# Neighbourhood attention: two heads at a time on both halves of the array, negated logits, and two pairs of logits moved into the value projection

## What is computed

```python
def row_block(r):                       # each of the 4 rows of the 64-wide grid
    rs = jnp.clip(r - kh // 2, 0, rows_n - kh)
    s_nb = jnp.einsum('bchd,bicjhd->bhcij', q_r, k_win).reshape(B, NA_HEADS, GRID_W, kh * NA_KW)
    s_nb = s_nb + bias[None]
    s_cx = jnp.einsum('bchd,blhd->bhcl', q_r, k_c)
    p = jax.nn.softmax(jnp.concatenate([s_nb, s_cx], axis=-1).astype(jnp.float32), axis=-1)
    ...
    return jnp.einsum('bhcij,bicjhd->bchd', p_nb, v_win) + jnp.einsum('bhcl,blhd->bchd', p_cx, v_c)
```

## Time and profile before

| | us |
|---|---|
| median of three runs | 2557.35 (2555.93 to 2558.05) |
| the profiled execution | 2556.38 |
| its span, first to last instruction | 2554.7 |
| first score matmul to first matmul of the output projection | 935.62 to 1032.93 |
| PE busy in the span | 2092.2 (82%) |
| DVE busy | 910.2 (36%) |
| ACT busy | 674.2 (26%) |
| DMA, mean over the span | 232 GB/s, and 418 GB/s from 1700 to 2550 |

### The profile page before, as it was taken

One profiled execution on the slowest core, in us unless ns is written; L12 is line 12 of the kernel. 1 busy time (PEld: TensorE's weight loads), 2 busy tenths in 40 slices (PEclk: granted clock), 3 DMA queues, 4 the chain that ended last, 5 costly groups with the idle time before them and its releaser, 6 DMA issues.

```text
span 2554.7 us, 37430 instructions
## 1 busy us (share of the span) xinstructions
PE 2092.2 (82%) x16374; PEld 1521.7 (60%) x16374; DVE 910.2 (36%) x1632; ACT 674.2 (26%) x1171; POOL 56.3 (2%) x83
## 2 busy tenths in 40 slices
PE   6997998999998989999989999666666666666655
PEld 4895645888776875799879445533344343333332
DVE  2335623444423227466365533423311111211112
ACT  4234313233314326455355211111111111111111
POOL 0011100000000011000000000000000000000000
PEclk8998999999998989999989999788878888888888
DMA  7107741222222321153631035599999999999997
GB/s 318 67 34 299 299 180 51 95 99 79 68 101 99 117 100 48 70 195 126 222 134 42 1 155 197 228 427 427 426 427 427 427 426 427 427 427 426 427 427 298
DMA packets 44433, 592.11 MB, mean 232 GB/s; under 512 B 5528, under 2 KB 5717, under 8 KB 8176
## 3 DMA queue, kind: packets, MB, share of 16 engines
q1 hardware_dynamic: 40608, 579.36, 55.5%
q0 software_dynamic: 2880, 8.45, 1.0%
q10 hardware_dynamic: 784, 1.91, 0.2%
HBM read 588.64 MB, written 1.05 MB: 231 GB/s over the span
## 4 chain that ended last, share of the span: by engine, by line
PE 53%; DMA 27%; DVE 4%; ACT 2%; issue 2%; SPq 0%; POOL 0%; DVEq 0%; ACTq 0%
DMA s_ring<-in_w_up 12%; PE bank L510 10%; PE bank L511 10%; PE bank L512 10%; DMA s_arena<-in_w_up 8%; PE bank L1079 5%; DMA s_hT<-in_w_up 4%; DMA s_xT<-in_w_up 3%; PE bank L1093 2%; PE bank L992 1%; PE bank L929 1%; PE bank L743 1%; PE bank L798 1%; PE bank L788 1%; PE bank L495 1%
## 5 line engine op out<-in xcount | busy, mean ns | idle before, releaser
L510 PE MATMUL bank<-s_arena_r 128*128 128x256 f32 (+2 forms) x1656 | 543.9, 328 | 37.0 <-DVE s_hT_r L1765 29.6
L1200 ACT ACTIVATE s_arena<-bank 32x256 f32<-32x256 f32 (+6 forms) x455 | 180.4, 404 | 1101.2 <-PE bank L1079 572.1
L512 PE MATMUL bank<-s_arena_r,s_ring_r 128*128 128x512 f32 (+2 forms) x1312 | 440.9, 336 | 0.0
L1079 PE MATMUL bank<-s_ring,s_arena 128*32 128x256 f32 x2048 | 299.8, 507 | 137.4 <-DMA s_hT<-in_w_up 45.3
L510 PEld LDWEIGHTS bank<-s_arena_r 128*128 128x128 f32 x1656 | 314.2, 190 | 73.8 <-issue 36.3
L1760 DVE TENSOR_TENSOR s_ring_r<-s_ring,s_arena_r 128x2048 fp32r<-128x2048 f32 (+1 forms) x96 | 232.5, 2425 | 306.7 <-ACT s_arena_r L1200 306.7
L511 PE MATMUL bank<-s_hT_r,s_arena_r 128*128 128x512 f32 (+1 forms) x904 | 314.8, 348 | 0.0
L1079 PEld LDWEIGHTS bank<-s_ring,s_arena 128*32 128x32 f32 x2048 | 147.8, 144 | 215.5 <-issue 202.6
L512 PEld LDWEIGHTS bank<-s_arena_r,s_ring_r 128*128 128x128 f32 x1312 | 252.6, 192 | 26.0
L1200 ACT ACTIVATE s_arena_r<-s_ring 128x2048 fp32r<-128x2048 f32 (+1 forms) x96 | 193.3, 2018 | 137.2 <-PE bank L512 136.4
L2286 DVE TENSOR_TENSOR s_arena<-s_arena,bank 64x256 f32<-64x256 f32 x64 | 27.1, 423 | 543.8 <-ACT s_arena L1200 543.8
(11 more groups left out here) (311 smaller groups left out, 2884.3 us busy)
## 6 DMA issues: line engine op xcount, KB each, us to landing
s_ring<-in_slabs SPq DMA_DIRECT2D x72, 2048.0 KB, 8.2
s_ring<-in_w_down SPq DMA_DIRECT2D x32, 2048.0 KB, 28.8
s_ring<-in_w_up SPq DMA_DIRECT2D x32, 2048.0 KB, 33.4
s_ring<-in_w_gate SPq DMA_DIRECT2D x32, 2048.0 KB, 33.4
s_arena<-in_w_gate SPq DMA_DIRECT2D x16, 2048.0 KB, 33.0
s_arena<-in_w_up SPq DMA_DIRECT2D x16, 2048.0 KB, 33.7
s_arena<-in_w_down SPq DMA_DIRECT2D x16, 2048.0 KB, 28.9
s_ring<-in_slabs SPq DMA_DIRECT2D x16, 1408.0 KB, 6.3
```

The lines of the kernel that those rows point to most:

```text
L510: mm(out, w_hi_, x_hi_, start=start, stop=False)
L512: return mm(out, w_lo_, x_hi_, start=False, stop=stop)
L1079: last = mm(pb[b][32 * q:32 * q + 32, 0:256], x[:, c, :], w[q // 2][:, c, 256 * (q % 2):256 * (q % 2) + 256], start=c == 0, stop=c == DC - ...
L1200: return act.activation(out, in_, func, **kw)
```

## The change

- The tiles come in 16 pairs `j`: one tile each of an even and an odd head, with the same query tile (`na_tile`). On PE the two score matmuls of a pair stand side by side, on the two halves of the rows, into two of now four banks. The two tiles' out matmuls alternate, on the two halves of the columns, into one bank, and one ACT instruction reads both.
- DVE makes the negated logits (minus logits minus bias) in one `scalar_tensor_tensor` and takes their minimum; exp runs with scale -1. The negation at L1988 is gone.
- The scores of pairs 0 and 1 stand in the value projection, behind its quarters k = 8 and k = 9; their adds stand on DVE ahead of and behind the last `half_lo`, and their exps on ACT ahead of the last four copies of v. The bias buffers are cleared and loaded from the end of FFN 1 on.
- PE's order per pair is: transposes of both tiles of pair j, scores of pair j+2, out of pair j-1. DVE's: both shares of pair j, both adds of pair j+2.
- Buffers: `n_s` and `n_pt` of four tiles, carved so that they are clear of what the value projection still reads.

```diff
-            pool.wait_ge(S["na_v_mm"], 16)
+            pool.wait_ge(S["ffn_out_mm"], DC)
...
+            def na_scores(j):
+                for a in range(2):
+                    i = 2 * j + a
+                    h, qt = na_tile(i)
+                    if i >= 4:
+                        pe.wait_ge(S["na_add"], i - 3)
+                    mm(NA_BANK[i % 4][:, :], n_q[64 * a:64 * a + 64, h // 2, 128 * qt:128 * qt + 128], n_k[64 * a:64 * a + 64, h // 2, :],
+                       start=True, stop=True).then_inc(S["na_s_mm"], 1)
+
+            def na_out(j):
+                pe.wait_ge(S["na_pt"], 2 * j + 2)
+                if j >= 2:
+                    pe.wait_ge(S["na_o_ev"], j - 1)
+                for k in range(4):
+                    for a in range(2):
+                        i = 2 * j + a
+                        h, qt = na_tile(i)
+                        last = mm(pb[j % 2][64 * a:64 * a + 64, 0:128], n_v[:, k, 64 * h:64 * h + 64], n_pt[:, i % 4, 128 * k:128 * k + 128],
+                                  start=k == 0, stop=k == 3, skip_group_check=True)
+                last.then_inc(S["na_o_mm"], 1)
...
+                if k in (8, 9):
+                    na_scores(k - 8)
             pe.wait_ge(S["na_v_ev"], 8)
...
+            def na_exp(i):
+                act.wait_ge(S["na_max"], i + 1)
+                A(n_s[i % 4], n_s[i % 4], ACT.Exp, scale=-1.0, bias=n_mx[:, i % 4, 0:1], accum_out=n_rs[:, i % 4, 0:1]).then_inc(S["na_exp"], 1)
...
+            for u in range(8):
+                if u >= 4:
+                    na_exp(u - 4)
+                copy("na_v_mm", 8 * (u // 4) + 4 + u % 4 + 1, "na_v_ev", pb[u % 4][:, :], n_v[:, u % 4, 512 * (u // 4):512 * (u // 4) + 512])
             for i in range(2 * NA_H):
+                if i >= 2 and i + 2 < 2 * NA_H:
+                    na_exp(i + 2)
                 act.wait_ge(S["na_tr"], i + 1)
+                if i >= 4:
+                    act.wait_ge(S["na_o_mm"], i // 2 - 1)
+                A(n_pt[:, i % 4, :], pb[2 + i % 2][:, :], ACT.Copy).then_inc(S["na_pt"], 1)
+                if i >= 2 and i % 2 == 0:
+                    na_read(i // 2 - 1)
...
-                TTn(n_s[:, i % 3, :], NA_BANK[i % 3][:, :], n_bias[:, i % 4, :], ALU.add).then_inc(S["na_add"], 1)
+                STT(out=n_s[i % 4], in0=NA_BANK[i % 4][:, :], scalar=-1.0, in1=n_bias[:, i % 4, :], op0=ALU.mult, op1=ALU.subtract).then_inc(S["na_add"], 1)
                 dve.wait_ge(S["na_add"], i + 1)
-                step(dve.tensor_reduce(n_mx[:, i % 3, 0:1], n_s[:, i % 3, :], AX_X, ALU.max))
-                TS(n_mx[:, i % 3, 1:2], n_mx[:, i % 3, 0:1], -1.0, None, ALU.mult).then_inc(S["na_max"], 1)
+                dve.tensor_reduce(n_mx[:, i % 4, 0:1], n_s[i % 4], AX_X, ALU.min).then_inc(S["na_max"], 1)
```

More of the change, by code:

```diff
@@ L247, in build, with na_tile @@
         t = carve()
-        n_q, n_k, n_v, n_o = t(DC, NT), t(DC, TT), t(4, D), t(DC, NT)
-        n_bias, n_s, n_pt = t(4, TT), t(3, TT), t(2, TT)
-        n_mx, n_rs = t(3, 4), t(3, 4)
+        n_q, n_k, n_v, n_bias, n_s01 = t(DC, NT), t(DC, TT), t(4, D), t(4, TT), t(2, TT)
+        assert t.at[0] <= f_at
+        n_o, n_pt = t(DC, NT), t(4, TT)
+        t.at[0] = f_at + DC * TT
+        n_s23, n_mx, n_rs = t(2, TT), t(4, 4), t(4, 4)
+        assert t.at[0] <= w_at
+        n_s = [n_s01[:, 0, :], n_s01[:, 1, :], n_s23[:, 0, :], n_s23[:, 1, :]]
+        def na_tile(i):
+            return 2 * (i // 4) + i % 2, i // 2 % 2
         hflat = hT[:, :, :].rearrange("p a b -> p (a b)")
@@ L780, in _ @@
                     last.then_inc(S["na_v_mm"], 1)
+                if k in (8, 9):
+                    na_scores(k - 8)
             pe.wait_ge(S["na_v_ev"], 8)
[L783 to L815, removed]
+            for j in range(NA_H):
+                for a in range(2):
+                    i = 2 * j + a
+                    pe.wait_ge(S["na_p"], i + 1)
+                    if i >= 2:
+                        pe.wait_ge(S["na_pt"], i - 1)
+                    for k in range(4):
+                        last = pe.transpose(pb[2 + a][:, 128 * k:128 * k + 128], n_s[i % 4][:, 128 * k:128 * k + 128], ident)
+                    last.then_inc(S["na_tr"], 1)
+                if j + 2 < NA_H:
+                    na_scores(j + 2)
+                if j >= 1:
+                    na_out(j - 1)
+            na_out(NA_H - 1)
+            pe.wait_ge(S["na_o_ev"], NA_H)
             project("na_out", lambda k: n_o[:, k, :], NT, 2 * DC, 1, "n2_1")
@@ L1473, in _ @@
                     copy("na_k_mm", u - 7, "na_k_ev", pb[u % 4][:, :], n_k[:, u - 8, :])
[L1474 to L1479, removed]
             def na_exp(i):
                 act.wait_ge(S["na_max"], i + 1)
-                A(n_s[:, i % 3, :], n_s[:, i % 3, :], ACT.Exp, bias=n_mx[:, i % 3, 1:2], accum_out=n_rs[:, i % 3, 0:1]).then_inc(S["na_exp"], 1)
@@ L1485, in na_read @@
[L1485 to L1490, removed]
+                A(n_s[i % 4], n_s[i % 4], ACT.Exp, scale=-1.0, bias=n_mx[:, i % 4, 0:1], accum_out=n_rs[:, i % 4, 0:1]).then_inc(S["na_exp"], 1)
+            def na_read(j):
+                act.wait_ge(S["na_o_mm"], j + 1)
+                h, qt = na_tile(2 * j)
+                A(n_o[:, h // 2, 128 * qt:128 * qt + 128], pb[j % 2][:, 0:128], ACT.Copy).then_inc(S["na_o_ev"], 1)
@@ L1975, in _ @@
                 h_rest(2, c, hT[:, c, :], hT_r[:, c, :], h_hi[:, c, :])
-            for k in range(1, 12):
-                half_lo(k, "na")
             def na_add(i):
```

42 lines of the change are left out of this document (24 added, 18 removed).

## The result

The changed kernel took 2565.44 us (median; lowest 2561.72, highest 2567.84) where the kernel before, beside it on the same chip, took 2559.11. The ratio is 1.0028, with a 95% interval from 1.0018 to 1.0037: slower by 0.28%, or 7.2 us, with an interval of 4.6 to 9.5. One of the seven executions of the kernel before took 3095.42 us; the ratio leaves it out, and the two medians as they stand differ by 6.3. The forecast was 2566.0, a little slower, and the range 2551 to 2576.

A forecast was written before the change was run, and what follows sets the result against it. PE bound the old attention loop. Attention at full clock, 92.9 us, plus 12.9 for the clock gave 105.8, 8.5 more than before; 2556.38 + 8.5 = 2564.9, and 0.97 for the median made 2566, range 2551 to 2576.

The forecast's parts named there:

- The cause: Attention loop: DVE waits a 1.80 us round trip per pair for scores; a 2.55 us gap on PE costs the clock.
- The halves: PE in attention: both array halves work at once, a pair of scores taking 1.05 us and its out 1.02.
- The value projection: PE in the value projection: two pairs of scores 2.1 us, plus 0.2 for changes between full array and halves; 2.3.
- One pair on DVE: DVE per pair: two adds with reduces 2.80 us, shares 1.29; the saved negation about pays for the slower 748 ns add.
- The cycle at full clock: Attention loop, per pair: round trip 1.80, adds 2.80 and shares 1.29 make 5.89 us, against 5.32 before.
- The clock: Attention loop: clock swings between full and half, cycle 6.80 us, 11.9 more over 13 cycles; chance 0.62.
- The sum: Whole attention: 92.9 us at full clock plus 12.9 for the lower clock, 105.8, or 8.5 more than before.
- To the end: Behind the attention: what it saves or loses reaches the kernel's end one to one, as the weight stream absorbs no delay.
- the prediction's own list: Signs of a wrong forecast: pair pitch under 5.3 us, short DVE wait for scores, or attention and kernel ends moving differently.
- A full clock: Rival, attention loop: the clock stays full, holding with gaps below about 2 us; 4.4 us less, 2553; chance 0.20.
- The halves don't overlap: Rival, PE in the attention loop: no overlap in the new order, cycle 6.6 us, 10.0 more, 2567; chance 0.04.
- DVE never waits for scores: Rival, attention loop: DVE runs at its own pace, 4.02 us a pair, giving 2529; faster than the old loop, chance 0.06.

The follow-up runs named there:

- scores ahead: The changed kernel with PE issuing the scores of pair j+2 ahead of the transposes of pair j; 2529.6 us, ratio 0.9892.
- the filled gap: The changed kernel with three more matmuls on PE behind the out of each pair, whose result nobody reads; 2549.36 us, ratio 0.9972.
- the old arithmetic with the scores ahead: The changed kernel with scores of pair j+2 ahead of transposes of pair j, and plain add, maximum and negation back on DVE; 2536.55 us, ratio 0.992.

## Why the prediction was right

The forecast of 2566.0 met 2565.44. I go through its steps.

*The cause.* The prediction named a round trip (share, transposes, scores, add) that the written order on PE puts into every cycle, and a gap on PE that costs the clock. Moving one call removed both and 36 us with them; keeping PE at work in the gap removed the second alone and 16 us. Both are shown. What exactly PE must do to keep the clock isn't: the dummies change the gap and the work together.

*The halves.* That they overlap is right: 1.13 for a pair of scores and 1.09 for out, beside 1.12 and 1.09 for one tile. The reading that led there was partly wrong. It took three scores in one half for 3.2 us, but two in one half take 1.98 in all, so three would be about 2.85. The 1.98 us of the three scores in the earlier trace rows is just the two of head 0, with that of head 1 beside them. The conclusion survives, the premise didn't.

*The value projection.* 2.3 us were forecast. The last matmul of v ends 0.69 ahead of the next work, at 937.12 against 934.93: 2.2. But what lies ahead moves that point by a microsecond or two from profile to profile, so the stretch has to be measured from its own start, the first matmul of the attention's projections. From 814.59 to 937.12 it is 122.5 us in the change and from 815.13 to 934.93 119.8 before. The other profiles agree: 122.2 to 122.8 with two halves at work in it, 119.8 and 120.3 without the scores. The price is 2.7, and the hit of 2.2 on 2.3 was chance.

*One pair on DVE.* The negated add was sized at 748 ns, by the 510-column form of the earlier trace rows. It took 0.68 to 0.69, the same as the plain add. Add to add is 1.33 and not 1.40. So the negation that is gone saves in full, 6 to 7 us, where I had written that it about pays for a slower add. This is the largest mistake of size: a form on other operands was taken for the price, in place of the plain add on the same operands.

*The cycle at full clock.* Forecast 5.89, measured 5.72. The 0.17 are the two adds and their handovers; over 13 cycles 2.2 us.

*The clock.* Taking the middle between 5.89 and 7.72, 6.80, was a choice, and 6.78 was measured. It is right partly by luck: the full cycle is shorter, only three of 13 are at the full clock, and the slow ones lie at 7.0 to 7.2, since each is at half the clock only in part. A cycle at half throughout takes 7.39, as the run without scores in the value projection has it (957.58 to 964.97), and not 7.72. The clock costs 1.06 a cycle and not 0.91, and the two errors cancel. The swing itself is as forecast: 0.81 over the loop, between the 0.6 and 0.9 that were named.

*The sum.* From the first transposes to the second 5.56, 13 cycles 88.1, and from the transposes at 1031.48 to the projection 9.5: 103.1, against a forecast of 105.8 - 2.3 = 103.5. Split where the forecast splits it, at the share of the second tile, that is 6.1 for 6.43, 88.1 for 88.5, and 8.9 for the tail's 7.6. The tail's 1.3 more are the half clock at its start, where an out takes 1.98; the 1.0 given for head and tail covers most of it.

*To the end.* I wrote that what the attention saves or loses reaches the end one to one. In the two profiled executions 8.0 us at its end became 5.2 at the end of the span. The next place that can be compared is the first matmul of the last stream (the min of start times, L1079 before and L1092 after; the first row is before):

```profile
L1079 PE MATMUL bank<-s_arena x1024: 376/604/636, 1621.3 to 2508.3; 128*32 128x256 f32 x171
```

```profile
L1092 PE MATMUL bank<-s_arena x1024: 376/631/636, 1625.0 to 2513.8; 128*32 128x256 f32 x171
```

There the difference is 3.7, so 4.3 us were given back between 1041 and 1625, and 1.5 added again in the stream. Of one stretch there, 1400 to 1500, the clock was 0.97 after and 0.93 before. No run tested why. By the prediction's own list, different amounts at the two ends are a sign of being wrong. But all ten profiles together bear the step out: the output projection starts anywhere from 1005.78 (scores ahead) to 1048.84 (no scores in the value projection), 43 us apart, and from there to the end of the span they take 1518.5 to 1522.0 us. What is gained or lost in the attention reaches the end to within 3.5 us, and that scatter holds the 2.8 that seem to be given back here.

*The rivals.* A full clock: made by the filled gap, 2549.4 for the 2553 forecast. The estimate that it would hold with gaps below about 2 us was too simple: with 1.76 in every cycle it held in some only, and of two single gaps of over 2, that of 2.44 kept it and that of 2.33 lost it (the old arithmetic with the scores ahead). The halves don't overlap: refuted. DVE never waits for scores: made by moving one call, 2529.6 for the forecast of 2529, though with a pitch of 4.17 and not 4.02. The Trainium skill says on the page "TensorEngine Tiling (Array Packing)", section "PSUM Bottleneck", that packing speeds up TensorE but not the reading of PSUM, which can then be the bottleneck; in that run the trace agrees as far as VectorE, busy 44.33 of 50 us, is now fuller than PE with 38.86. But only VectorE's two adds, 1.37 of its 3.9 us a pair, read PSUM; its minima and shares work in SBUF. In the change itself that rule wasn't what decided. The prediction was right to put the written order first.

## What to carry over

Before a loop is packed tighter on one engine, write out which result each engine waits for in turn: work that the other engine needs first has to stand first in the queue, and here one call in another place was worth 36 us, while the whole change without it lost 7, and some 14 against the kernel before with its bias early. Where a chain leaves TensorE waiting some 2 us in every cycle, add what a lower clock will cost to the price of the chain, and look whether other work, even useless work, shortens the gap. An engine's idle time says nothing about what an instruction on it costs; whether the next engine waits for that instruction does.

## What was not expected of the hardware

- A scalar_tensor_tensor that reads PSUM and SBUF over 512 columns took 0.68 to 0.69 us, the tensor_tensor on the same operands 0.69. The 748 ns of the earlier trace rows belong to another use of it.
- Two scores in a row on the same half took 1.98 us, one alone 1.12; a group of matmuls that follows its like is cheaper by 0.15 to 0.2 us than one behind another kind.
- The clock fell with gaps of 1.76 us in every cycle (0.90 from 950 to 1000) and not with gaps of 1.26 (1.00, the old arithmetic with the scores ahead), nor behind one gap of 2.44 at the start of that same run, though it did behind one of 2.33 at its end. The busy times of those 50 us, 37.24 and 36.10, mislead: the first holds work at half the clock, which takes longer. In a cycle at the full clock PE works 3.96 of 5.72 us in the one and 3.34 of 4.60 in the other, so the run with the longer gaps also works the smaller part of its time, and no run here tells the two apart.
- Putting two pairs of scores between the matmuls of the value projection cost 2.7 us on PE, where the pairs alone, at 1.06 from start to the next start, are 2.1.
